# DRAM-to-DRAM copies in rows of 8 and 10 KB, and the sample's values loaded two key tiles at a time

## The reference

```
proj = x @ w_in                                  # 1024 -> 4096
q, k, v, g_att, gb, gc, hh, g_conv = split(proj)
o_att = merge of three dilated window attentions (128,1), (512,4), (2048,16)
att   = o_att * silu(g_att)
z     = gb * conv3(gc * hh) * silu(g_conv)
y     = LayerNorm(2**0.25 * x + concat(att, z) @ w_out)
```

## Time and profile before

| | us |
|---|---|
| Median of 3 runs | 361.42 |
| Lowest and highest run | 359.41, 361.47 |
| Span of the profiled execution, first to last instruction | 356.6 |
| PE busy in the span | 347.5 |
| Bytes moved by DMA | 141.06 MB |

### The profile page before, as it was taken

The page is one execution under the profiler, slowest core; times in us unless marked ns, Lnnn a source line. Parts: engine busy times, 40 slices in busy tenths (PEclk is TensorE's granted clock), DMA queues, the critical chain, the costliest instruction groups (busy, mean ns, idle before and its releaser), DMA issues.

```text
span 356.6 us, 7735 instructions
## 1 busy us (share of the span) xinstructions
PE 347.5 (97%) x3290; PEld 312.2 (88%) x3290; DVE 201.2 (56%) x379; ACT 117.3 (33%) x231; POOL 10.6 (3%) x28
## 2 busy tenths in 40 slices
PE   7999999999999999999999999999999999999992
PEld 5998988899998888999988889999788998888782
DVE  4534438854134649561346573821456499877775
ACT  5523324342144233421332423412533635230000
POOL 0000000000100000001000000000000000300000
PEclk9999999999999999999999999999999999999998
DMA  8999999999999999999999999999999999999992
GB/s 299 403 422 414 417 417 417 418 421 420 418 396 418 417 416 381 369 422 385 411 408 415 421 414 420 427 421 419 421 412 413 415 417 371 399 364 347 361 364 112
DMA packets 34549, 141.06 MB, mean 396 GB/s; under 512 B 3410, under 2 KB 3794, under 8 KB 32466
## 3 DMA queue, kind: packets, MB, share of 16 engines
q1 hardware_dynamic: 18050, 73.20, 51.0%
q10 hardware_dynamic: 16464, 67.37, 47.9%
HBM read 135.80 MB, written 71.86 MB: 582 GB/s over the span
## 4 chain that ended last, share of the span: by engine, by line
PE 96%; DVE 1%; DMA 1%; DVEq 0%; ACT 0%; issue 0%
PE pj_a L1137 11%; PE pj_b L1137 10%; PE pj_b L1139 10%; PE pj_a L1138 10%; PE pj_b L1138 10%; PE pj_a L1139 10%; PE sc L1261 5%; PE sc L1297 5%; PE px L1209 3%; PE po L1241 3%; PE px L1454 3%; PE px L1456 3%; PE px L1455 3%; PE pt L1227 2%; PE pt L1281 1%; DMA k_buf<-in_first 1%
## 5 line engine op out<-in xcount | busy, mean ns | idle before, releaser
L1137 PE MATMUL pj_a<-x_hi,w_hi 128*128 128x288 f32 x256 | 78.1, 305 | 1.2 <-DVE x_lo L779 1.2
L1137 PE MATMUL pj_b<-x_hi,w_hi 128*128 128x288 f32 x256 | 77.5, 303 | 0.0
L1138 PE MATMUL pj_a<-x_lo,w_hi 128*128 128x288 f32 x256 | 75.5, 295 | 0.0
L1138 PE MATMUL pj_b<-x_lo,w_hi 128*128 128x288 f32 x256 | 75.5, 295 | 0.0
L1139 PE MATMUL pj_b<-x_hi,w_lo 128*128 128x288 f32 x256 | 75.4, 294 | 0.0
L1139 PE MATMUL pj_a<-x_hi,w_lo 128*128 128x288 f32 x256 | 75.3, 294 | 0.0
L1137 PEld LDWEIGHTS pj_a<-x_hi,w_hi 128*128 128x128 f32 x256 | 48.0, 187 | 8.5 <-issue 6.2
L467 ACT CAST w_hi<-w_raw 128x1024 fp32r<-128x1024 f32 x30 | 31.4, 1046 | 65.5 <-PE pj_b L1139 32.8
L773 DVE TENSOR_TENSOR w_lo<-w_raw,w_hi 128x1024 fp32r<-128x1024 f32 x30 | 36.7, 1223 | 28.7 <-ACT w_hi L467 28.7
L1137 PEld LDWEIGHTS pj_b<-x_hi,w_hi 128*128 128x128 f32 x256 | 48.0, 187 | 2.3 <-issue 1.3
L1139 PEld LDWEIGHTS pj_b<-x_hi,w_lo 128*128 128x128 f32 x256 | 48.2, 188 | 0.0
(11 more groups left out here) (153 smaller groups left out, 434.9 us busy)
## 6 DMA issues: line engine op xcount, KB each, us to landing
k_buf<-in_k_used SPq DMA_DIRECT2D x16, 1280.0 KB, 13.8
v_buf<-in_v_used SPq DMA_DIRECT2D x40, 512.0 KB, 19.0
out_k_used_out<-in_k_used ACTq DMA_DIRECT2D x16, 1280.0 KB, 17.2
out_v_used_out<-in_v_used ACTq DMA_DIRECT2D x20, 1024.0 KB, 16.9
w_raw<-in_w_tiles SPq DMA_DIRECT2D x30, 512.0 KB, 13.0
out_k_rest_out<-in_k_rest ACTq DMA_DIRECT2D x12, 1024.0 KB, 11.6
out_v_rest_out<-in_v_rest ACTq DMA_DIRECT2D x12, 1024.0 KB, 12.7
wo_raw<-in_w_out SPq DMA_DIRECT2D x8, 512.0 KB, 20.9
```

What stands on the lines that cost most here:

```text
L1137: nc.tensor.matmul(out, w_hi[:, w], x_hi[:, c], start=(k == 0), stop=False)
L1138: nc.tensor.matmul(out, w_hi[:, w], x_lo[:, c], start=False, stop=False)
```

## The change

Three things are different. The copies of the rest of the cache are cut in 8 rows of 8 KB for each of 16 parts (the DRAM tensors get rows of 2048 numbers). The used keys are copied in their own rows of 10 KB. The used values are laid out in DRAM with two key tiles in a row of 8 KB, are copied in such rows and are loaded by five DMAs of 1 MB a round in place of ten of 512 KB; each has one semaphore, so that `sample_values` waits for a pair. The number of copies, their bytes, and the places in ACT's list where they are issued are the same, and so is the space of `v_buf`.

```diff
-V_SLOTS = V_PIECES
+V_LOADS = V_PIECES // 2
+REST_COLS = 2048
...
-            def load_v(i, n):
-                n += V_PIECES * i
-                slot = n % V_SLOTS
-                if n >= V_SLOTS:
-                    sp.wait_ge(v_used, n - V_SLOTS + 1)
-                sp.dma_start(v_buf[:, slot * 1024:(slot + 1) * 1024],
-                             d["v_used"][n * P:(n + 1) * P, :]).then_inc(v_in[slot], 16)
+            def load_v(i, m):
+                n = V_LOADS * i + m
+                if i:
+                    sp.wait_ge(v_used, V_PIECES * (i - 1) + 2 * m + 2)
+                sp.dma_start(v_buf[:, m * 2048:(m + 1) * 2048],
+                             d["v_used"][n * P:(n + 1) * P, :]).then_inc(v_in[m], 16)
...
-            def short_runs(rows):
-
-                if rows.shape[1] == K_SLOT:
-                    rows = rows.rearrange("r (m n) -> (r m) n", m=2)
+            def by_sixteenths(rows):
+
                 return rows.rearrange("(r a) n -> a r n", a=16)
 
             def copy_rest(n):
                 name = ("k_rest", "v_rest")[n % 2]
-                rows = slice(n // 2 * 256, (n // 2 + 1) * 256)
-                act.dma_start(short_runs(d[name + "_out"][rows, :]), short_runs(d[name][rows, :])).then_inc(copied, 16)
+                rows = slice(n // 2 * P, (n // 2 + 1) * P)
+                act.dma_start(by_sixteenths(d[name + "_out"][rows, :]), by_sixteenths(d[name][rows, :])).then_inc(copied, 16)
...
             def copy_v(i, s):
-                rows = slice((V_PIECES * i + 2 * s) * P, (V_PIECES * i + 2 * s + 2) * P)
-                act.dma_start(short_runs(d["v_used_out"][rows, :]), short_runs(d["v_used"][rows, :]))\
+                rows = slice((V_LOADS * i + s) * P, (V_LOADS * i + s + 1) * P)
+                act.dma_start(by_sixteenths(d["v_used_out"][rows, :]), by_sixteenths(d["v_used"][rows, :]))\
                     .then_inc(copied, 16)
...
             def sample_values(i, t):
 
-                n = V_PIECES * i + t
                 ends = t == V_PIECES - 1
...
-                pe.wait_ge(v_in[n % V_SLOTS], 16 * (n // V_SLOTS + 1))
+                pe.wait_ge(v_in[t // 2], 16 * (i + 1))
...
-    a["v_used"] = v_used.reshape(DEC_BATCH, V_PIECES, P, NHP, P).transpose(3, 1, 2, 0, 4)\
-        .reshape(NHP * V_PIECES * P, 1024)
-    a["k_rest"], a["v_rest"] = (r.reshape(REST_ROWS * 256, 1024) for r in (k_rest, v_rest))
+    a["v_used"] = v_used.reshape(DEC_BATCH, V_LOADS, 2, P, NHP, P).transpose(4, 1, 3, 2, 0, 5)\
+        .reshape(NHP * V_LOADS * P, 2048)
+    a["k_rest"], a["v_rest"] = (r.reshape(REST_ROWS * P, REST_COLS) for r in (k_rest, v_rest))
```

More of the change, by code:

```diff
@@ L129, in layer_step @@
         pt_s = sb("pt_s", [P, (USED_TILES + 1) * P], stack=early)
-        v_buf = sb("v_buf", [P, V_SLOTS * 1024], stack=early)
+        v_buf = sb("v_buf", [P, V_PIECES * 1024], stack=early)
         o_pr = sb("o_pr", [P, SEQ], stack=early)
@@ L155, in layer_step @@
         k_in = [sem(f"k_in{n}") for n in range(K_PIECES)]
-        v_in = [sem(f"v_in{n}") for n in range(V_SLOTS)]
+        v_in = [sem(f"v_in{n}") for n in range(V_LOADS)]
         k_saved, v_saved, vn_saved, copied, conv_out = (
@@ L338, in _ @@
                 load_w(t0 + 3)
-                for n in range(0, 3):
-                    load_v(i, n)
+                load_v(i, 0)
                 load_w(t0 + 4)
-                for n in range(3, 6):
-                    load_v(i, n)
+                load_v(i, 1)
+                load_v(i, 2)
                 load_w(t0 + 5)
-                for n in range(6, 8):
-                    load_v(i, n)
+                load_v(i, 3)
                 load_w(t0 + 6)
-                for n in range(8, 10):
-                    load_v(i, n)
+                load_v(i, 4)
                 load_w(t0 + 7)
@@ L360, in _ @@
             load_w(W_TILES - 2)
[L361 to L364, removed]
+            load_v(NPAIR - 1, 0)
+            load_v(NPAIR - 1, 1)
             def load_wo(n):
@@ L374, in _ @@
             load_wo(0)
-            load_v(NPAIR - 1, 4)
-            load_v(NPAIR - 1, 5)
+            load_v(NPAIR - 1, 2)
             load_w(W_TILES - 1)
@@ L379, in _ @@
             load_wo(1)
-            load_v(NPAIR - 1, 6)
-            load_v(NPAIR - 1, 7)
+            load_v(NPAIR - 1, 3)
             sp.wait_ge(k_used, pieces + 3)
             load_wo(2)
-            load_v(NPAIR - 1, 8)
-            load_v(NPAIR - 1, 9)
+            load_v(NPAIR - 1, 4)
             sp.wait_ge(k_used, pieces + 4)
@@ L420, in _ @@
             sp.wait_ge(conv_out, 16)
-            sp.wait_ge(copied, 16 * (2 * REST_ROWS + NPAIR * (K_PIECES + V_PIECES // 2)))
+            sp.wait_ge(copied, 16 * (2 * REST_ROWS + NPAIR * (K_PIECES + V_LOADS)))
         @block.gpsimd
@@ L490, in copy_rest @@
                 name = ("k_rest", "v_rest")[n % 2]
-                rows = slice(n // 2 * 256, (n // 2 + 1) * 256)
-                act.dma_start(short_runs(d[name + "_out"][rows, :]), short_runs(d[name][rows, :])).then_inc(copied, 16)
+                rows = slice(n // 2 * P, (n // 2 + 1) * P)
+                act.dma_start(by_sixteenths(d[name + "_out"][rows, :]), by_sixteenths(d[name][rows, :])).then_inc(copied, 16)
             def copy_k(i, c):
                 rows = slice((K_PIECES * i + c) * P, (K_PIECES * i + c + 1) * P)
-                act.dma_start(short_runs(d["k_used_out"][rows, :]), short_runs(d["k_used"][rows, :]))\
+                act.dma_start(by_sixteenths(d["k_used_out"][rows, :]), by_sixteenths(d["k_used"][rows, :]))\
                     .then_inc(copied, 16)
             def copy_v(i, s):
-                rows = slice((V_PIECES * i + 2 * s) * P, (V_PIECES * i + 2 * s + 2) * P)
-                act.dma_start(short_runs(d["v_used_out"][rows, :]), short_runs(d["v_used"][rows, :]))\
+                rows = slice((V_LOADS * i + s) * P, (V_LOADS * i + s + 1) * P)
+                act.dma_start(by_sixteenths(d["v_used_out"][rows, :]), by_sixteenths(d["v_used"][rows, :]))\
                     .then_inc(copied, 16)
-            copies = iter(range(2 * REST_ROWS + NPAIR * (K_PIECES + V_PIECES // 2)))
+            copies = iter(range(2 * REST_ROWS + NPAIR * (K_PIECES + V_LOADS)))
             def copy_next():
@@ L515, in copy_next @@
                     n -= 2 * REST_ROWS + NPAIR * K_PIECES
-                    copy_v(n // (V_PIECES // 2), n % (V_PIECES // 2))
+                    copy_v(n // (V_LOADS), n % (V_LOADS))
             def stage_v(i):
@@ L1292, in sample_values @@
                     pe.wait_ge(s_masked, K_PIECES * (i + 1))
-                pe.wait_ge(v_in[n % V_SLOTS], 16 * (n // V_SLOTS + 1))
+                pe.wait_ge(v_in[t // 2], 16 * (i + 1))
                 for b in range(2):
                     for r in range(NPAIR):
-                        v0 = n % V_SLOTS * 1024 + (2 * r + b) * P
+                        v0 = t * 1024 + (2 * r + b) * P
                         last = nc.tensor.matmul(sc[r * 32:r * 32 + 32, b * P:(b + 1) * P],
@@ L1563 @@
         .reshape(DEC_BATCH, USED_TILES, P, D_ATT)
-    v_used = r["v_used_out"].reshape(NHP, V_PIECES, P, DEC_BATCH, P).transpose(3, 1, 2, 0, 4)\
+    v_used = r["v_used_out"].reshape(NHP, V_LOADS, P, 2, DEC_BATCH, P).transpose(4, 1, 3, 2, 0, 5)\
         .reshape(DEC_BATCH, USED_TILES, P, D_ATT)
```

## The result

| | before | after |
|---|---|---|
| Median of 20 runs each, us | 361.39 | 365.07 |
| Lowest and highest, us | 358.72, 363.9 | 362.47, 370.08 |
| Span of the profiled execution, us | 356.6 | 362.9 |
| The profiled execution's own time, us | not on the page | 364.73 |

The changed kernel takes 1.0097 times as long (95% interval 1.0081 to 1.0113): 3.5 us more, where 1.0 us was forecast. Where the time went, the page and the windows show.

A forecast was written before the change was run, and what follows sets the result against it. The prediction took PE to bound the kernel, with DMA equally full but not waited for. Span 356.6 + 0 + 1.0 + 0 = 357.6 us, with the median 4.8 us above: 362.4 us, range 359.2 to 366.2.

The forecast's parts named there:

- What bounds the kernel: Between 7 and 350 us PE waits only 0.17 us, so DMA time saved brings 0 to -0.2 us, taken as 0.
- rival B: Faster: DMA sets the pace after all, and 7.7 us less of it shortens the end, giving 353.7 us; chance 0.03.
- The base: Profiled span 356.6 us; the median of runs lies 4.8 us above it, and that difference stays after the change.
- How the queues share: While q10 and q1 both have work, they take turns packet by packet, so bytes go by row length.
- rival A: Slower: PE starved of weights, tile 24 landing 7.9 us late, 4.8 over what it bears, giving 366.2 us; chance 0.15.
- The saving: Fewer packets free 7.7 us of every DMA engine's time in all, 1.4 us of it before tile 24.
- The price of a packet: On a DMA engine, 36.6 ns for each KB and 12 ns for the packet itself, 15 by another point.
- Later weights: Longer copy rows make tile 24 at most 4.1 us late; it bears 3.1, so PE waits +1.0 us (0 to +6.2).
- the cap of 5.5: Tile 24's lateness is limited by 2.3 MB unserved in q10 when it lands: 5.5 us at 416 GB/s, before the saving.
- The end: The last stores come later, but only lateness over 1.2 us counts: 0 taken, bounds 0 and +2.9 us.
- rival D: The end pays: the store is late by its full cap, +2.9 us, giving 364.3 us; chance 0.05.
- Rival C: Engines cut the 8 and 10 KB rows into 4 or 5 KB, so nothing changes: 361.4 us; chance 0.04.

The follow-up runs named there:

- pairs with 8 KB rows for the rest: Changed kernel with value copies cut to 4 KB and key copies to 5 KB, the rest's copies in 8 KB, values loaded in pairs: 358.28 us, 0.9935 to before.
- pairs alone: Changed kernel with all copies cut back to 4 and 5 KB rows, values loaded in pairs: 359.69 us, 0.9965 to before; repeated, 360.48 us, 0.9983.
- doubled rows: Changed kernel with all copy rows doubled, to 16 KB for rest and values and 20 KB for keys: 375.35 us, 1.0275 to before.
- the other three kernels with 10 KB key copies: Kernel before with key copies alone lengthened, 364.62 us; changed kernel with tile 24's load issued earlier, 363.37; or one round-2 copy behind its split, 365.7.
- short key copies: Changed kernel with key copies cut back to 5 KB rows, rest and values still in 8 KB, value loads in pairs: 361.06 us, 1.0013 to before.

## Why the prediction was right or wrong

**What bounds the kernel: half right.** PE sets the end in both, and the loss is a PE wait for late weights plus what follows it. But the "0.17 us" of waiting was read from one of the fastest executions. The other one profiled, near the median, waits for output weights behind 294 us. That the DMA engines' time cannot come back (rival B) was therefore too strong: pairs with 8 KB rows for the rest win 0.65% against the kernel before. By what path, and whether the rest's rows have a part in it, is not settled: that kernel's profile (span 356.4) looks like the first one of before. A hint is the slow start, after which the kernel before waited for output weights and pairs alone did not, in one profile each.

**The base: wrong reading, harmless.** "The median of the runs is 4.8 us above this execution's span, and that stays." What lies around a span is 1.8 us (364.73 - 362.9; 362.44 - 360.6). The other 3.0 us are the difference between a fast and a middling execution, so the reserve at each step was that of a fast one, too.

**How the queues share: right where both have work, only there.** From 228 to 238 us, in the changed kernel (answers to the earlier trace rows):

```profile
q10 hardware_dynamic: 262, 2.39, 57.3%
q1 hardware_dynamic: 271, 1.74, 42.9%
```

Equal packets, and the bytes now lean to the copies, where before they leaned to the loads. From 186 to 200 us (answers to the earlier trace rows):

```profile
q1 hardware_dynamic: 672, 3.42, 59.3%
q10 hardware_dynamic: 265, 2.43, 41.3%
```

Here q10 has far fewer: ACT, waiting 6.9 us for tile 21, could not issue copies. This is the give-back that the prediction held against rival A, and it is real. It comes too late: the loads that it serves first are keys and values, and tile 24 was issued at 197.2 us in place of 192.5, because SP waits for DVE's split of tile 22, itself late. Lateness is handed on from tile to tile through the two slots of `w_raw`.

**The saving: this term failed, while the price behind it holds.** "The saving of about ten copies and eight value pieces has come in: 1,800 x 12 / 16 = 1.4 us." In sum it did not come in. DMA queues from 150 us to the split of tile 24, the kernel before (to 212.52) and then the changed one (to 219.16):

```profile
q10 hardware_dynamic: 2984, 14.05, 55.5%
q1 hardware_dynamic: 2666, 11.52, 45.7%
```

```profile
q10 hardware_dynamic: 1726, 15.46, 55.6%
q1 hardware_dynamic: 2277, 12.16, 45.0%
```

With all queues that is 25.68 MB at 411 GB/s before and 27.72 MB at 401 after: at 411 they would have taken 67.4 us in place of 69.2, so 1.7 us were lost where 1.4 were to be saved. The price of a packet is not what was wrong. By the line of 36.6 ns for each KB and 12 ns for the packet, the changed kernel's copies from 186 to 200 us (9.17 KB on average) should take 348 ns, and take 41.3% of 224 us over 265 = 349 ns; from 228 to 238 us (9.12 KB) 346, and take 350; with doubled rows from 190 to 200 us (17.8 KB) 662, and take 665. Most of what was lost lies in one stretch, 176 to 187 us, where the changed kernel moved 345 GB/s and the one before 411:

```profile
q10 hardware_dynamic: 289, 2.59, 66.5%
q1 hardware_dynamic: 341, 1.19, 34.0%
```

Here packets of both queues take longer than the line says: q10's 405 ns for 8.96 KB (340 by the line), q1's 175 ns for 3.5 KB (140). It is deepest from 182 to 186 us: 287 GB/s, and 325, 315 and 308 in the other three kernels with 10 KB key copies, against 407 to 417 in the two profiles of the kernel before, with short key copies and with pairs alone. So the long key rows bring it about, but the length of a packet alone does not explain it, for such dips occur with 4 KB rows too (343 GB/s from 320 to 330 us in the kernel before). Its cause is open. (The "15 ns" beside the 12, too, does not come out of the rows that it names: the packets of 251 and 78 ns give 12.6. It only served a bound.)

**Later weights: the place and the reserve right, the sum too small.** Tile 24 was 6.6 us late, not 4.1. From 150 us to its split q10 had moved 1.4 MB more than before: 3.4 us at 411 GB/s, within the cap of 5.5. q1 had moved 0.6 MB more: 1.6 us, for which the prediction had no term. The lower rate took 1.7 us, where the prediction counted 1.4 us the other way. 3.4 + 1.6 + 1.7 = 6.7. It can bear 3.1 us, said the prediction; 6.6 - 3.1 = 3.5, and PE waited 3.65. Tile 25 was 2.1 us late (223.39 for 221.31), as worked out (2.0), and cost nothing, as said; but that is luck, for with the key copies alone in long rows tile 24 was 2.9 us late (215.38), and tile 25 5.8 (227.10), and there PE paid. "Delays of PE shift all that follows and are not added up": not so for tile 28, whose split stands before y_pad: 1.0 us.

**What had no term at all: the clock.** After the wait of 3.65 us PE ran at 1.2 GHz from 223.2 to 226.6 us: 1.7 us.

**The end: right.** DVE's timeline at the end of the changed kernel (answers to the earlier trace rows):

```profile
352.58 0.69 DVE L1074 SCALAR_TENSOR_TENSOR y_t<-x_res,px 128x512 f32<-128x512 f32 x1 [2.06 <-DMA out_y<-y_t]
...
356.34 0.42 DVE L1093 SCALAR_TENSOR_TENSOR y_t<-x_res,sc 128x256 f32<-128x256 f32 x1 [1.51 <-PE sc L1445]
```

DVE still waits last for PE: rival D is out. The end pays only in the two extremes, with copy rows of 16 and 20 KB and of 2 and 2.5 KB.

**Rival A** came near in time (366.2, measured 365.07), and its sign is there: PE idle over 3 us with pj_a named. Its cause is not. It took the 3.8 us that the load at 85.8 us waited for packets already taken up, twice as long with rows twice as long: 6.4 + 3.8 + 1.2 (its own turns) = 11.4 us. In the changed kernel, issued at 85.5 us:

```profile
w_raw<-in_w_tiles SPq DMA_DIRECT2D x1, 512.0 KB, 8.2
```

With the rest in 8 KB and all else short it is 6.1 us, with rows of 2 KB 6.7. That is not an order by row length. The rule of the Trainium skill ("DMA: Bandwidth & Descriptors", Queues, rings and completion order) that an engine drains 9 to 17 descriptors of a queue before it switches stood behind A; these loads do not bear out a cost from it here. **Rival C** is out by the packets.

## What to carry to other kernels

When two queues share the DMA engines, the length of a row is its queue's share of the bytes: lengthen the rows of what somebody waits for, and keep those of background copies short (here 4 to 5 KB) wherever loads have no reserve; where they have it, longer copies cost nothing. Shorten them no further without a look at the engine that issues them: at 2 and 2.5 KB the weights came in time, and the issues held ACT up. Price a late load at every consumer behind it in the order of each engine, not at the first, for curing one moves the wait to the next, and add what the clock takes after a wait. And read the reserve from a middling execution: when the profiled span lies well under what the median minus the time around the span gives, it shows more slack than most runs have.

## What the runs showed of the hardware

- While both queues had work, SP's and ACT's queues had equal packets, whatever their length: 691 and 690, 366 and 367, after the change 262 and 271. ACT's waits for weight tiles were 2.0, 30.5 and 53.1 us in all with key copies in rows of 2.5, 5 and 10 KB (in the last with the values loaded in pairs, which alone give 9.7).
- The issue of one copy held ACT for 0.61 us in the kernel before at 215.55 us, and for up to 7.82 us with rows of 2.5 KB (one profile, of an execution above its median). Why is open.
- After a PE wait of 3.65 us the matmuls went from 0.13 to 0.24 us apart from 223.2 to 226.6 us; after one of 3.9 us about 3.0 us of work were lost; after waits of 1.5 us there was none, after one of 1.94 us 1.7 us (0.58 over 4 us). What else stood before each fall is not told apart.
- One and the same kernel began with matmuls 0.24 us apart (until about 10.5 us) in one profile and 0.13 us apart in another: 1.6 us of its scatter. The Trainium skill ("TensorE: Matmul & The Clock Gate", Part 1: The HAM clock gate) says that the number of slow matmuls at a kernel's start varies between runs of the same kernel; by that rule, these two traces agree.
- Throughput over 7 to 340 us did not rise with rows over 4 to 5 KB (407, 401 GB/s) and was lower with 2 to 2.5 KB (392, in an execution above its median), although the DMA share read 1.00 to 1.02 in all; from 182 to 186 us in the changed kernel 287 GB/s stand beside a share of 1.00. The share doesn't tell how well the engines are used.
